# Expert blocks gathered further ahead into three buffers, and the last stage's sums moved to VectorE

## What is computed

```python
def run_block(xb, e):                        # rows xb of h, gathered by expert
    return (silu(xb @ w_eg[e]) * (xb @ w_eu[e])) @ w_ed[e]
...
y_a = ys[dest] * gate                        # each pair's row times its gate
f = zeros((T, D)).at[tok].add(y_a)           # two rows added per token
y = layer_norm(DN_ALPHA * h + f, ln2_g, ln2_b)
```

## Time and profile before

| | |
|---|---|
| median of 3 runs | 3290.61 us |
| the profiled execution's own time | 3283.69 us |
| its span, first to last instruction | 3281.9 us |
| busy: TensorE, VectorE, ScalarE, GpSimd | 2780.1, 1827.7, 1033.3, 529.6 us |
| TensorE's mean granted clock | 0.936 |
| bytes moved by DMA | 303.11 MB |

### The profile page before, as it was taken

How to read it: one execution, slowest core, us unless ns; L and a number is a source line. 1 busy time by engine, 2 the same in 40 slices (tenths; PEclk the granted TensorE clock), 3 DMA queues, 4 the chain that set the end, 5 groups by cost and what they waited for, 6 DMA issues and landing times. The chain is left out here.

```text
span 3281.9 us, 69371 instructions
## 1 busy us (share of the span) xinstructions
PE 2780.1 (85%) x28140; PEld 2020.2 (62%) x28140; DVE 1827.7 (56%) x3864; ACT 1033.3 (31%) x2481; POOL 529.6 (16%) x525
## 2 busy tenths in 40 slices
PE   7999999999999997689898989899847777777850
PEld 6888888888888886555555555455434444344430
DVE  1666666666666666387786878322363323233328
ACT  2333333333333333143444444222202221222225
POOL 0000000000000000000000000011114333334436
PEclk9999999999999998699999999999869988888985
DMA  6111221121222214201000010355347786665335
GB/s 191 36 36 36 39 40 37 38 41 36 40 45 42 38 37 95 92 4 35 4 15 25 1 35 1 120 161 161 130 176 238 240 293 216 187 218 158 78 92 186
DMA packets 336905, 303.11 MB, mean 92 GB/s; under 512 B 236654, under 2 KB 291982, under 8 KB 322192
## 3 DMA queue, kind: packets, MB, share of 16 engines
q1 hardware_dynamic: 318016, 248.31, 25.4%
q0 software_dynamic: 18576, 50.36, 6.8%
HBM read 208.64 MB, written 85.47 MB: 90 GB/s over the span
## 5 line engine op out<-in xcount | busy, mean ns | idle before, releaser
L800 PE MATMUL mx_bank<-mx_xT,mx_w_in 128*128 128x128 f32 x5168 | 646.0, 281 | 18.4 <-DVEq L263 13.8
L800 PEld LDWEIGHTS mx_bank<-mx_xT,mx_w_in 128*128 128x128 f32 x5168 | 600.5, 193 | 62.0 <-issue 37.2
L2278 PE MATMUL ex_gate<-pl_wg,ex_xT 128*64 x768 | 221.4, 453 | 171.5 <-DVE ex_bg L2353 152.9
L2344 DVE STREAM_TRANSPOSE ex_xT<-ex_x 128x256 f32<-128x256 f32 x192 | 105.9, 608 | 453.9 <-DMA ex_x<-scr_hx,ex_plan 453.9
L2278 PEld LDWEIGHTS ex_gate<-pl_wg,ex_xT 128*64 128x64 f32 x768 | 123.8, 165 | 279.4 <-issue 245.9
L1483 PE MATMUL at_bank<-pl_kT,pl_qT 128*128 128x512 f32 (+5 forms) x656 | 289.6, 528 | 2.3 <-issue 2.3
L1455 ACT ACTIVATE at_PQ<-at_bank,at_nms 128x512 f32<-128x512 f32 (+5 forms) x328 | 193.0, 596 | 252.4 <-DVE at_nms L1583 250.9
L2209 POOL DMA_INDIRECT ex_x<-scr_hx,ex_plan x192 | 210.8, 1098 | 102.3 <-issue 57.9
L2279 PE MATMUL ex_gate<-ex_bg,ex_xT 128*64 128x256 f32 x768 | 221.5, 453 | 0.0
L1626 DVE COPY at_PT<-at_bank 128x512 f32<-128x512 f32 (+3 forms) x328 | 196.2, 599 | 44.7 <-PE at_bank L1495 28.1
L696 ACT ACTIVATE mx_pr<-mx_bank 128x256 f32<-128x256 f32 (+1 forms) x68 | 36.7, 541 | 554.4 <-PE mx_bank L800 471.9
(11 more groups left out here) (346 smaller groups left out, 5291.8 us busy)
## 6 DMA issues: line engine op xcount, KB each, us to landing
pl_wg<-in_w_eg SPq DMA_DIRECT2D x32, 1024.0 KB, 6.7
pl_wu<-in_w_eu SPq DMA_DIRECT2D x32, 1024.0 KB, 11.1
pl_wd<-in_w_ed SPq DMA_DIRECT2D x32, 1024.0 KB, 5.0
mx_x<-in_x SPq DMA_DIRECT2D x76, 128.0 KB, 3.8
scr_acc<-ro_blank SPq DMA_DIRECT2D x19, 512.0 KB, 6.2
pl_ro_x<-in_x SPq DMA_DIRECT2D x17, 512.0 KB, 5.4
scr_hx<-ro_h SPq DMA_DIRECT2D x17, 512.0 KB, 2.7
scr_acc<-ro_ha SPq DMA_DIRECT2D x17, 512.0 KB, 3.2
```

The source lines that it names most:

```text
L800: ins = pe.matmul(dst, w_in[:, k, col:col + n], xT[:, k, :], start=(k == 0), stop=(k == KC - 1))
L2278: pe.matmul(out[s][0:HB, 0:FE], xT[s][:, k, 0:HB], wv[:, c], start=(k == 0), stop=(k == KC - 1))
```

## The change

In `experts` there are three `x` buffers in place of two, and the two `xT` buffers stay. GpSimd issues the gathers of blocks 0 to 4 at the start (those of 3 and 4 wait for their buffers), and then for each i `add(i)`, `gathers(i+5)`. VectorE does `turned(i+1)` after `second_gate(i+1)`, where it did it before `silu(i)`.

In `combine` GpSimd no longer sums. It clears and gathers the tiles one after another, and VectorE adds whole tiles of 1024 columns. One semaphore, `summed_up`, takes the place of two.

```diff
@@ experts
-        x, xT, th, hid, hT, y = ([sb(f"{n}{s}", shape, dt) for s in range(2)] for n, shape, dt in (
-            ("x", [P, 4, FE], F32), ("xT", [P, KC, P], F32), ("th", [P, FE], F32),
-            ("hid", [P, FE], F32), ("hT", [P, FC, P], F32), ("y", [P, D], F32)))
+        NX = 3
+        x = [sb(f"x{k}", [P, 4, FE]) for k in range(NX)]
+        xT, th, hid, hT, y = ([sb(f"{n}{s}", shape) for s in range(2)] for n, shape in (
+            ("xT", [P, KC, P]), ("th", [P, FE]), ("hid", [P, FE]), ("hT", [P, FC, P]), ("y", [P, D])))
...
-        x_in = [Dmas(nc, ctx, f"ex_x_in{s}", 4) for s in range(2)]
+        x_in = [Dmas(nc, ctx, f"ex_x_in{k}", 4) for k in range(NX)]
...
             def gathers(i):
-                s = i % 2
-                if i >= 2:
-                    g.wait_ge(xT_made, i - 1)
+                s = i % NX
+                if i >= NX:
+                    g.wait_ge(xT_made, i - NX + 1)
...
-            for i in range(2):
+            for i in range(NX + 2):
                 gathers(i)
             for i in range(NBLK):
-                if i + 2 < NBLK:
-                    gathers(i + 2)
                 add(i)
+                if i + NX + 2 < NBLK:
+                    gathers(i + NX + 2)
...
             def turned(i):
-                s = i % 2
-                v.wait_ge(x_in[s].sem, x_in[s].done(i // 2))
+                s, k = i % 2, i % NX
+                v.wait_ge(x_in[k].sem, x_in[k].done(i // NX))
                 if i >= 2:
                     v.wait_ge(up_done, i - 1)
                 for h in range(4):
-                    ins = v.transpose(xT[s][:, :, 32 * h:32 * h + 32], x[s][:, h, :].rearrange("p (i k) -> p k i", k=KC))
+                    ins = v.transpose(xT[s][:, :, 32 * h:32 * h + 32], x[k][:, h, :].rearrange("p (i k) -> p k i", k=KC))
...
             for i in range(NBLK):
                 more = i + 1 < NBLK
-                if more:
-                    turned(i + 1)
                 silu(i)
                 if more:
                     at = second_gate(i + 1)
+                    turned(i + 1)
                 hidden(i)
@@ combine
             def bring(t):
                 k = t % NB
                 if t >= NB:
-                    g.wait_ge(low_summed, t - NB + 1)
-                    g.wait_ge(high_summed, t - NB + 1)
+                    g.wait_ge(summed_up, t - NB + 1)
...
-            for t in range(NB):
+            for t in range(NT):
                 bring(t)
-            for t in range(NT):
-                k = t % NB
-                g.wait_ge(c_in[k], 16 * (t // NB + 1))
-                g.wait_ge(r_in[k], 16 * (t // NB + 1))
-                g.tensor_tensor(r[k][:, 0:LOW], r[k][:, 0:LOW], c[k][:, 0:LOW], ALU.add).then_inc(low_summed, 1)
-                if t + NB < NT:
-                    bring(t + NB)
...
-                v.tensor_tensor(r[k][:, LOW:D], r[k][:, LOW:D], c[k][:, LOW:D], ALU.add).then_inc(high_summed, 1)
+                v.tensor_tensor(r[k][:], r[k][:], c[k][:], ALU.add).then_inc(summed_up, 1)
...
             def total(t):
                 k = t % NB
-                a.wait_ge(low_summed, t + 1)
-                a.wait_ge(high_summed, t + 1)
+                a.wait_ge(summed_up, t + 1)
```

More of the change, by code:

```diff
@@ L2396, in combine @@
     NB = 5
-    LOW = 512
     with ExitStack() as ctx:
@@ L2413, in combine @@
         o_out = [ctx.enter_context(nc.semaphore(f"co_o_out{k}")) for k in range(NB)]
-        cleared, low_summed, high_summed = (ctx.enter_context(nc.semaphore("co_" + name)) for name in
-                                            ("cleared", "low_summed", "high_summed"))
+        cleared, summed_up = (ctx.enter_context(nc.semaphore("co_" + name)) for name in
+                                            ("cleared", "summed_up"))
         summed, centred, squared, rooted, gained, inverted, done = (
```

## The result

| | before | after |
|---|---|---|
| median of 4 runs | 3290.39 us (3258.64 to 3292.5) | 3065.6 us (3062.32 to 3071.9) |
| the profiled execution's own time | 3283.69 us | 3062.32 us |
| its span | 3281.9 us | 3060.2 us |
| TensorE's mean granted clock | 0.936 | 0.957 |

The ratio is 0.934, with a 95% interval of 0.928 to 0.940. Of the profiled execution's own time, 3283.69, the change took 221.4 us off, where 172.7 were forecast (to 3111).

The account below looks back on a forecast made before the run. Late gathers in `experts`, holding up VectorE and then TensorE, were taken as the bound. From 3283.69, -156 (`experts`) and -17 (`combine`) gave 3111, or 3118 on the scale of the medians; range 3078 to 3168.

Parts of the forecast that it names:

- What bounds the kernel: In `experts`, late gathers (453.9 us of VectorE waits) and TensorE's 152.9 us waiting for `bg` form one chain.
- Gathers, VectorE's order, GpSimd: In `experts`: the gather wait goes; VectorE's 4.9 us behind a gate and GpSimd's 6.9 us a block cost nothing.
- the cover of 2.4 us: In `experts`: VectorE's transposes end about 4.9 us after a gate; TensorE needs them 7.3 us after it.
- one of my signs of being wrong: In `experts`: transposes end later than 7 us after a gate and TensorE waits for them.
- What is late next: `experts` stage: the larger of TensorE time and DMA work per stretch, at share 0.90, gives 551 us; term -156.
- a rival, at 15%: `experts`: DMA never binds; stage 505 to 532 us, -175 to -202, with `combine` 3072 to 3098; chance 15%.
- Weight waits: `experts`: weight loads have 15 to 26 us from issue to first use against 7.5 to 12.8 to landing; fit narrowly.
- this rival: `experts`: gather wait turns into weight wait as bursts delay loads; stage 602 to 634 us, kernel 3169 to 3201; chance 20%.
- `combine`: Last stage: whole-tile sums on VectorE give 3.72 us a tile and an earlier start; term -17, bounds -3 and -20.
- the lead of five tiles: In `combine`: GpSimd is up to five tiles ahead; without that cover, contention at 3.9 us a tile costs some 2 us.

Follow-up runs that it names:

- 1 MB more: Changed kernel with SyncE loading 1 MB more of `wd` per expert, from the fifth on, into an unused tile: 3097.88 us, ratio 0.946.
- 14.7 MB added: Changed kernel with SyncE loading 0.5 MB more of `wd` per expert, from the fifth on, into an unused tile: 3077.38 us, ratio 0.940.

## Why the prediction was wrong

**What bounds the kernel: right.** The chain from add to gathers to transposes to `bg` was the whole loss. The pair with two buffers, the old and the earlier gathers, shows it best: 682.3 us of stage against 512.9.

**Gathers, VectorE's order, GpSimd: right.** The wait for `x` was to fall below 30 us and is 7.9. VectorE's 4.9 us behind a gate are 4.7, and the cover of 2.4 us was used up once, at gate 18: the transposes ended 7.3 us after the gate and TensorE waited some 0.4 us, which was one of my signs of being wrong and cost no more than that. The new order itself brought nothing. GpSimd's 6.9 are 6.7. Block 1 was to cost 1 us and cost 2 (8.8).

**"What is late next": the step that failed.** The sum took "the larger of the two in each stretch", with "DMA work that doesn't shrink" at a share of 0.90, and gave 551 us for the stage. It measured 505.7, which is TensorE's own 505. Three things in it were wrong.

- The share. "A stretch can't keep all 16 engines busy to the last" was read from 0.86, where the engines had waited for the same gathers as all the rest. They held 1.00 for 174 us here, and 1.03 for 304 us with 1 MB more. A share reached in a stalled kernel is no ceiling. At a share of 1 the sum would have been 532.
- The work shrank. Length times share over the first four stretches was 378 us; now it is 88.9 + 86.7 + 86.9 + 90.5 = 353, for the same bytes (119.8 MB from the earlier trace rows, 119.3 now). Full engines moved 347 to 355 GB/s. Before, rate over share was 331, 310 and 306 GB/s in blocks 10 to 34. So the busy share isn't a measure of work that carries over. The byte is.
- The stretch is no wall. Blocks 10 to 17 moved 37.7 MB before (132.2 us at 285 GB/s) and 30.1 MB now (86.7 at 347). Nearly all of the other 7.6 MB were moved later: 5.4 MB more in blocks 18 to 25 and 1.8 MB more in 26 to 34. As I read it, TensorE used up loads that four slots had fetched early, and the slots filled again while the experts changed less often. The bytes by stretch show the shift; that three slots cost 27.5 us in this stretch shows that the lead is needed, by late loads and not by full engines.

Together these account for 45 of the 49 us by which the forecast of 3111 missed the profiled execution's 3062.32: 19 by the share (551 to 532), 26 by the stretches taken one by one and the work taken as fixed (532 to 505.7), which the runs don't part further. I had this case as a rival, at 15% and 3072 to 3098, and the result lies 6 us below even that: by 1.6 of `combine`, 1.3 of the way into it, and a median only 3.3 us above the profiled execution, where I had added 6.9. "For it" stood there that the four stretches' DMA work, 378 us, is just under TensorE's 375. It is just over, but the comparison over all four was the right one. Its upper half still came from the wall between stretches.

**Weight waits: right.** Forecast to fit narrowly, they did: 12.4 us on VectorE, of which some 0.4 reached TensorE as a wait for transposes. The landing grew from 12.8 to 20.6 us at most, which this rival had said, but not to where it costs. With three slots it does cost 58.1 us of waits. That is the rival's mechanism, one slot away.

**`combine`: right.** A tile takes 3.72 us, as worked out. From the first memset, `gain` of tile 1 comes 6.0 us earlier (forecast 5.0), that of tile 2 6.4 (5.4), nine tiles save 8.6 (8.6), and from `gain` of tile 11 to the end it is 24.7 us in place of 28.2, -3.5 (-4 + 1.6). In all -18.6 for -17. The Trainium skill (SBUF — State Buffer, "Who interferes with whom") says that a VectorE instruction with two SBUF inputs contends with a GpSimd instruction that reads SBUF; whether issuing a gather counts as one, this rule doesn't say. By it I had estimated 3.9 us a tile, should the lead of five tiles not cover it. A gather took 1.99 us beside VectorE's operations where it took 1.00 while VectorE stood, which agrees in kind with being blocked for one of them. One gather (at 2999.68) took 1.00 beside a `shift` that had begun 0.1 us before, so the rule isn't shown to hold each time. VectorE's operations stayed at 1.22 and 1.28 us, the tile at 3.72, and the lead covered the longer gathers.

## What to carry to other kernels

When a stall goes, cost the transfers behind it by bytes, at the rate that full queues reach, and over as many blocks as the buffers reach ahead; neither a busy share read in the stalled kernel nor a stretch between two marks is a limit. Here that says rightly that the DMA engines don't bind: 119.3 MB at 372 GB/s are 321 us against TensorE's 375. It is a first estimate and no more, since with 14.7 MB added it came out 11 us too low. Then ask how much lead is left: some 30 us of room in 271 by the estimate above, and one buffer slot less cost 44.5. And before adding buffers, look where in its engine's list the issue stands: between two kernels that differ in that alone the stage went from 682 to 513 us, and the third buffer gave 7 more.

## What the hardware showed that I had not expected

- All 16 DMA engines held full share for 304 us with weight loads, gathered rows and scattered adds mixed, at 372 GB/s; the engines moved 306 to 331 GB/s for each full share in the stalled kernel's blocks 10 to 34 (with 1 MB more, a larger part of the bytes are large loads).
- Full engines lengthened the landing of a 1 MB `wu` load, issued right behind `wg`, from a median of 11.4 to 13.5 us, with a tail of 20.6; that of `wd` grew from 4.9 to 9.1.
- The kernel before varies by 36 us between runs (3258.64 to 3294.23) and the changed one by 12. The stage with the old gathers took 707.4 us in one profile and 685.3 in another kernel's, with the same instructions in the stage.
- GpSimd's memset of a whole tile (0.97 us) took its usual time beside VectorE's sums and cost VectorE nothing, while GpSimd's own sum of half a tile had lengthened `gain` from 1.28 to 2.77 us.
- A gather that adds into the tile took 1.88 us to issue on average, and landed in time for a pace of 3.06 us a tile.
